# Output stages of a 1-core Trainium2 kernel: the last two weight units taken token half by token half, the norm behind them by halves too

## What is computed

```
first_block:                       # adaptive RMS norms, scale and shift from c
  h = rms(x) * (1 + scale) + shift;  x += gate * (hybrid_mixer(h) @ hyb_w_out)
  h = norm(x);                       x += gate * (swiglu(h) @ ffn_w_out[0])
  h = norm(x);                       x += gate * (retention(h) @ ret_w_out)
  h = norm(x);                       x += gate * (swiglu(h) @ ffn_w_out[1])
second_block, l = 0, 1:
  mix = concat(rms(y_lru), rms(y_nsa)) @ w_out[l]
  x = layer_norm(ALPHA * x + mix, ln1)
  x = layer_norm(ALPHA * x + peer(x), ln2)      # peer: 128 experts, out = sum_e c_e @ v_e
```

## Time and profile before

| what | value |
|---|---|
| profiled execution, its own time | 3087.28 us |
| its span | 3085.5 us |
| median of three runs | 3087.29 us |
| TensorE matmul busy | 2828.8 us (92%) |
| VectorE busy | 2225.6 us (72%) |
| ScalarE busy | 1604.9 us (52%) |
| mean granted TensorE clock | 0.954 of full |

### The profile page before, as it was taken

The page is one execution under the profiler, slowest core; times in us unless marked ns, Lnnn a source line. Parts: engine busy times, 40 slices in busy tenths (PEclk is TensorE's granted clock), DMA queues, the critical chain, the costliest instruction groups (busy, mean ns, idle before and its releaser), DMA issues.

```text
span 3085.5 us, 46430 instructions
## 1 busy us (share of the span) xinstructions
PE 2828.8 (92%) x17816; PEld 2520.9 (82%) x17816; DVE 2225.6 (72%) x3602; ACT 1604.9 (52%) x2733; POOL 82.9 (3%) x141
## 2 busy tenths in 40 slices
PE   6888799899799997999999999989798999999997
PEld 3675599786699876989999888878698999988886
DVE  2753566676555555899898878874579998977887
ACT  2333244334344353467888554545445778855453
POOL 1000000010000200000000000020000000000000
PEclk8889899899899988999999999998799999999999
DMA  7323567576355623556656877763255656587775
GB/s 254 111 62 116 191 226 252 181 230 206 116 178 182 208 77 102 182 186 204 193 190 205 265 241 242 241 207 117 70 178 180 202 189 198 190 264 242 243 241 161
DMA packets 211610, 580.28 MB, mean 188 GB/s; under 512 B 24032, under 2 KB 87808, under 8 KB 210112
## 3 DMA queue, kind: packets, MB, share of 16 engines
q1 hardware_dynamic: 162704, 495.20, 50.4%
q0 software_dynamic: 12976, 49.60, 4.9%
q10 hardware_dynamic: 35712, 32.52, 3.1%
HBM read 541.57 MB, written 35.65 MB: 187 GB/s over the span
## 4 chain that ended last, share of the span: by engine, by line
PE 73%; DVE 17%; ACT 6%; issue 2%; DMA 1%; ACTq 0%; POOL 0%; DVEq 0%; POOLq 0%
PE psum L692 72%; DVE wr L1895 4%; DVE gmem L1895 4%; DVE oh_r L1895 3%; ACT gmem L1352 2%; DVE gmem L1898 2%; ACT wr L1352 2%; ACT crf L1352 1%; PE psum L735 1%; DVE xmem L1898 1%; ACT L1352 1%; DVE gmem L2663 1%; DVE gmem L2076 0%; ACT xmem L1352 0%; ACTq L1838 0%
## 5 line engine op out<-in xcount | busy, mean ns | idle before, releaser
L1895 DVE TENSOR_TENSOR wr<-raw,wr 128x1024 fp32r<-128x1024 f32 (+1 forms) x814 | 994.2, 1223 | 494.5 <-ACT wr L1352 492.6
L692 PE MATMUL psum<-xr,wr 128*128 128x256 f32 x10464 | 1314.4, 286 | 31.0 <-DVE wr L1895 14.8
L692 PEld LDWEIGHTS psum<-xr,wr 128*128 128x128 f32 x10464 | 1289.3, 195 | 44.9 <-DVE xr L1895 14.5
L1352 ACT ACTIVATE wr<-raw 128x1024 fp32r<-128x1024 f32 (+1 forms) x814 | 853.8, 1049 | 320.7 <-PE psum L692 271.5
L692 PE MATMUL psum<-wr,cr 128*128 128x512 f32 x3072 | 696.8, 389 | 3.0 <-DVE cr L1895 3.0
L692 PEld LDWEIGHTS psum<-wr,cr 128*128 128x128 f32 x3072 | 576.6, 188 | 122.7 <-ACT cr L1352 3.3
L1352 ACT ACTIVATE gmem<-psum 128x512 f32<-128x512 f32 (+2 forms) x307 | 162.0, 540 | 276.2 <-PE psum L692 242.4
L1352 ACT ACTIVATE cr<-xmem 128x256 fp32r<-128x256 f32 x256 | 107.2, 419 | 341.9 <-PE psum L692 339.9
L692 PE MATMUL psum<-wr,xr 128*128 128x512 f32 (+1 forms) x960 | 242.3, 410 | 21.0 <-DVE xr L1895 11.0
L692 PEld LDWEIGHTS psum<-wr,xr 128*128 128x128 f32 x960 | 184.5, 200 | 68.3 <-issue 15.0
L692 PE MATMUL psum<-gmem 128*128 128x128 f32 (+8 forms) x1352 | 196.1, 299 | 17.2 <-DVE gmem L1895 13.6
(11 more groups left out here) (143 smaller groups left out, 1652.8 us busy)
## 6 DMA issues: line engine op xcount, KB each, us to landing
raw<-in_uv SPq DMA_DIRECT2D x512, 512.0 KB, 4.8
raw<-in_ffn_in SPq DMA_DIRECT2D x88, 512.0 KB, 4.1
gs<-xmem ACTq DMA_DIRECT2D x248, 128.0 KB, 3.7
xmem<-gs SPq DMA_DIRECT2D x248, 128.0 KB, 4.5
raw<-in_ada_w SPq DMA_DIRECT2D x48, 512.0 KB, 4.0
gmem<-in_ada_w POOLq DMA_DIRECT2D x48, 512.0 KB, 4.7
raw<-in_ffn_out SPq DMA_DIRECT2D x44, 512.0 KB, 3.5
raw<-in_ret_a SPq DMA_DIRECT2D x32, 512.0 KB, 4.3
```

Source lines behind the costliest of these rows:

```text
L692: ins = pe.matmul(o, a, b, start=first and i == 0, stop=final and i == len(pairs) - 1, skip_group_check=skip)
L1352: return act.activation(o, a, func, **k)
L1895: return dve.tensor_tensor(o, a, b, op)
```

## The change

The last two units of each output stage are multiplied together by a new function: first both units for token half 0, then both for token half 1. After the first of these TensorE raises a new signal, "half". VectorE's `residual`, or the first part of `layer_norm`, takes half 0 on that signal and half 1 on the end of the last unit. Variance, root and reciprocal are done for each half by itself. In `ada_norm` the row is first multiplied by the scale row (tensor_tensor, no need of the root), then by the reciprocal with the shift added, in two pieces of 512, each of which TensorE can transpose. ScalarE loads the table of the square root some units before the end of the stage (`preload_act_table`) in `hybrid_out`, `ffn_out_` and `peer_v`. VectorE's `split()` of the last unit's step goes behind the norm as `split(0)`, and so do the two clearings. The output is written by two DMAs.

```diff
+        def out_last(b, c_of, ks, sig):
+            pair = [(k, *next_unit()) for k in ks]
+            for a in range(2):
+                for k, j, hi, lo in pair:
+                    for n in range(2):
+                        e = slice(512 * n, 512 * n + 512)
+                        ch, cl = c_of(k)
+                        ins = mm3(bank(b + 2 * a + n), [(ch[:, quarter(a)], cl[:, quarter(a)], hi[:, e], lo[:, e])],
+                                  False, k == ks[1], True)
+                    if a:
+                        ins.then_inc(*W.pe.up(j))
+                    elif k == ks[1]:
+                        ins.then_inc(*X.pe.up(("half", sig)))
...
@@ tensor_program @@
         def hybrid_out(k):
-            out_unit(0, xr, k, 0, 8)
+            if k < 6:
+                out_unit(0, xr, k, 0, 8)
+            elif k == 6:
+                out_last(0, rows_of(xr), (6, 7), "hyb out")
...
         def peer_v(l, e):
+            c = e % 2
+            if e == NEXP - 2:
+                pe.wait_ge(*X.dve["c", l, NEXP - 1])
+                out_last(0, lambda k: (ccr[:, k % 2, 0, :], ccr[:, k % 2, 1, :]), (NEXP - 2, NEXP - 1), ("l2", l))
+            if e >= NEXP - 2:
+                return
...
         def mix_start(l):
-                    pe.wait_ge(*X.dve["ffn out", 1, 3])
                     for g in range(2):
+                        pe.wait_ge(*X.dve["ffn out", 1, 2 * a + g])
...
@@ scalar_program @@
         def ada_norm(tag):
             for a in range(2):
+                if name:
+                    act.wait_ge(*X.dve[(*name, 2 * a + 1)])
                 f(h[:, a, :], x[:, a, :], AF.Square, accum_out=ss[:, a:a + 1]).then_inc(*N.act.up((tag, "sq", a)))
-            root(N, tag, ss)
+            for a in range(2):
+                act.wait_ge(*N.dve[tag, "var", a])
+                f(ss[:, a:a + 1], ss[:, a:a + 1], AF.Sqrt).then_inc(*N.act.up((tag, "root", a)))
...
@@ vector_program @@
         def ada_norm(tag):
+            for a in range(2):
+                v = ss[:, a:a + 1]
+                dve.wait_ge(*N.act[tag, "sq", a])
+                ts(v, v, 1.0 / D, EPS, ALU.mult, ALU.add).then_inc(*N.dve.up((tag, "var", a)))
+                tt(h[:, a, :], x[:, a, :], aa, ALU.mult).then_inc(*N.dve.up())
+                dve.wait_ge(*N.act[tag, "root", a])
+                dve.reciprocal(v, v).then_inc(*N.dve.up())
                 own(N)
+                for g in range(2):
+                    e = slice(512 * g, 512 * g + 512)
+                    stt(h[:, a, e], h[:, a, e], v, sh[:, e], ALU.mult, ALU.add).then_inc(*N.dve.up((tag, "h", a, g)))
             for a in range(2):
                 for g in range(2):
                     lo_of(tag, xr, a, g, 4 + 2 * a + g)
+            if tag == ("ffn", 0):
+                zero(ff_b, [P, 2, 512]).then_inc(*A.dve.up(("zero", 0)))
...
+            if tag != "hyb":
+                split(0)
...
+        def residual(name, gt, tmp):
+            ahead.step()
+            for a in range(2):
+                dve.wait_ge(*(done() if a else X.pe["half", name]))
...
         def layer_norm(tag, src, g, b_, split_):
+            for a in range(2):
+                dve.wait_ge(*(done() if a else X.pe["half", tag]))
...
+                own(X)
                 for i in range(2):
                     dve.bn_stats(st[:, a, 6 * i:6 * i + 6], src[:, a, 512 * i:512 * i + 512]).then_inc(*N.dve.up())
...
+                ts(mv[:, 2 * a + 1:2 * a + 2], mv[:, 2 * a + 1:2 * a + 2], 1.0, LN_EPS, ALU.mult,
+                   ALU.add).then_inc(*N.dve.up((tag, "var", a)))
+            for a in range(2):
+                dve.wait_ge(*N.act[tag, "root", a])
+                dve.reciprocal(mv[:, 2 * a + 1:2 * a + 2], mv[:, 2 * a + 1:2 * a + 2]).then_inc(*N.dve.up())
...
@@ sync_program @@
+        for a in range(2):
+            sp.wait_ge(*N.dve[("l2", 1), "x", a])
+            sp.dma_start(out[128 * a:128 * a + 128, :], x[:, a, :]).then_inc(out_sem, 16)
```

More of the change, by code:

```diff
@@ L107, in call @@
         return self
-    wait_ge = matmul = transpose = activation = memset = tensor_tensor = tensor_scalar = call
+    wait_ge = matmul = transpose = activation = memset = tensor_tensor = tensor_scalar = preload_act_table = call
     scalar_tensor_tensor = tensor_copy = reciprocal = tensor_reduce = bn_stats = bn_aggr = call
@@ L318, in __init__, with step @@
             self.unit, self.next = -1, 0
+        def step(self):
+            self.unit += 1
         def to_split(self, step=1):
@@ L1074, in ret_out_ @@
                 claim(0, 1, 2, 3)
-            out_unit(0, oT, k, 0, 16)
+            if k < 14:
+                out_unit(0, oT, k, 0, 16)
+            elif k == 14:
+                out_last(0, rows_of(oT), (14, 15), "ret out")
             for i in range(4):
@@ L1558, in hybrid_out @@
             split()
+            if k == 4:
+                act.preload_act_table(AF.Sqrt)
         def mods(part):
@@ L1769, in layer_norm @@
         def layer_norm(tag, src, g, b_, split_):
-            root(N, tag, small_v[:, 24:28].rearrange("p (a s) -> p a s", s=2)[:, :, 1])
+            for a in range(2):
+                v = small_v[:, 25 + 2 * a:26 + 2 * a]
+                act.wait_ge(*N.dve[tag, "var", a])
+                f(v, v, AF.Sqrt).then_inc(*N.act.up((tag, "root", a)))
             if split_:
@@ L2028, in ada_norm @@
                     lo_of(tag, xr, a, g, 4 + 2 * a + g)
[L2030 to L2033, removed]
+            if tag == ("ffn", 0):
+                zero(ff_b, [P, 2, 512]).then_inc(*A.dve.up(("zero", 0)))
+            if tag == "ret":
+                zero(re_b, [P, 2, 512]).then_inc(*A.dve.up(("zero", 1)))
+            if tag != "hyb":
+                split(0)
         def qkv_(p, i):
@@ L2245, in hybrid_out @@
         def hybrid_out(k):
-            split()
-            if k == 7:
-                residual("hyb out", top(0), hy_tmp, done())
+            if k < 7:
+                split()
+            else:
+                residual("hyb out", top(0), hy_tmp)
         def mods(part):
@@ L2289, in ffn_out_ @@
         def ffn_out_(l, k):
-            split()
-            if k == FM - 1:
+            if k < FM - 1:
+                split()
+            else:
                 if l:
                     dve.wait_ge(*A.act["row", 11])
-                residual(("ffn out", l), top(3 if l == 0 else 9), ff_h, done())
+                residual(("ffn out", l), top(3 if l == 0 else 9), ff_h)
         def ret_qk(p, i):
@@ L2356, in ret_out_ @@
         def ret_out_(k):
-            split()
-            if k == 15:
-                residual("ret out", top(6), re_tmp, done())
+            if k < 15:
+                split()
+            else:
+                residual("ret out", top(6), re_tmp)
         def mix_start(l):
@@ L2533, in mix_out @@
         def mix_out(l, k):
-            split()
-            if k == 7:
-                dve.wait_ge(*done())
-                dve.wait_ge(*S.dve[("on", l), "rstd"])
-                for i in range(4):
-                    a = i // 2
-                    v = my[:, a, 512 * (i % 2):512 * (i % 2) + 512]
-                    stt(v, bank(2 + i), rn[:, 2 + a:3 + a], v, ALU.mult, ALU.add).then_inc(*X.dve.up(("mix out", l, i)))
+            if k < 7:
+                split()
         def layer_norm(tag, src, g, b_, split_):
@@ L2743, in peer_v @@
                 halve(l, e + 1)
-            split()
+                split()
         def peer_end(l):
-            dve.wait_ge(*done())
-            dve.wait_ge(ln2_in[l], 48)
-            for i in range(4):
-                a, e = i // 2, slice(512 * (i % 2), 512 * (i % 2) + 512)
-                stt(x[:, a, e], xo[:, a, e], ALPHA, bank(i), ALU.mult, ALU.add).then_inc(*X.dve.up(("y", l, i)))
+            pass
         order({"prologue": prologue, "modulate": modulate, "ada_norm": ada_norm, "qkv": qkv_, "conv": conv,
```

57 lines of the change are left out of this document (32 added, 25 removed).

## The result

The changed kernel takes 3065.83 us (median of five executions, 3064.67 to 3068.6). The kernel before has a median of 3100.83 over five executions (3086.4, 3087.29, 3100.83, 3103.18, 3104.34), three of them the ones that the prediction had. The ratio over all these executions is 0.9904, with a 95% interval of 0.9874 to 0.9933 (the quotient of the two medians would be 0.9887). So the change is faster by about 1%, but its time lies above the range of 3050 to 3064: the forecast was 3056.7. The profiled execution of the kernel after took 3065.82, span 3064.0, against a span of 3085.5 before. From profile to profile the change gives 21.5 us where the sum had 30.6.

What follows compares the result with a forecast made beforehand. Mostly TensorE matmuls (73% of the chain of waits); winnable time lies in joints, as long as VectorE's chain. 17.1 + 5.2 + 4.4 + 2.6 + 0.9 + 0.4 = 30.6 off 3087.3 gives 3056.7 us; range 3050 to 3064.

Steps and rivals of the forecast that it cites:

- joint 1: Gap behind the first output stage: first transposes at T + 5.1, TensorE restarts at T + 11.6 instead of 16.9, gain 5.3.
- output's DMA: Behind joint 8: the last DMA carries 512 KB and not 1 MB, gain 0.9, between 0.6 and 2.05.
- first norm: Order by halves adds a pass over the row but lets transposes start by pieces: gain 0.4, bounds 0 and 0.8.
- wait in `peer_v`: Ahead of joints 6 and 8: TensorE's pair waits for the multiplier of unit 127, 1.0 us lost in each.
- pair in the other joints: No cost to TensorE: 0.3 us to spare in joints 1 to 4, some 0.1 in joints 5 and 7.
- the 0.1 that was left out: Joints 1 to 3: uncertainty of the three-operand 512 piece, 0.65 to 0.68, 0.1 per joint, taken at the lower end.
- I take both, they cancel: Clock at two restarts: joint 4 probably stays at full clock, 1.6 gained; joint 6 falls to 0.50, 1.6 lost.
- The clock is kept: Rival: shorter gaps leave TensorE at full clock at four more restarts, 6.4 less, 3050 us; chance 0.12.
- ScalarE in VectorE's place: Rival: ScalarE's queue or a lost table preload delays joints 1 to 3 by 1.28 each, 3060.5 us; chance 0.08.
- Late loads: Rival: raw and `aux` loads fall together behind the joint, 0.7 to 1.9 in seven joints, 3062 to 3070; chance 0.08.
- Half 0 not overlapped: Rival: VectorE comes late to the signal, seven halves of 2.7 missing, 19 more, 3075.7 us; chance 0.06.
- The restart starves: Rival: the load released by deferred `split(0)` comes too late for units 5 and 6, 3103 us; chance 0.03.

Runs made afterwards that it cites:

- experiment 6: Changed kernel without the three preloads of the square root's table: median 3069.97 us, ratio 0.9905 to the kernel before.
- experiment 1: The kernel before, unedited, measured and profiled once more: median 3099.31 us over 12 executions, ratio 0.9996.
- experiment 7: Changed kernel plus unread TensorE products in the waits of joints 1 to 3 and 5 to 7, nine or twelve ahead of the transposes: median 3066.98 us.
- the same, late waits (8): experiment 7 plus, in the pair, later waits for the last `peer_v` multiplier and the second unit's lo part: median 3064.88 us, ratio 0.9887.
- Experiment 9: The kernel of (8) with fewer unread products, five or six ahead of the transposes, sized by the measured call: median 3046.54 us, ratio 0.9836.
- experiment 5: Changed kernel with VectorE's `split()` put back in front of the residual and the norm: median 3092.72 us, ratio 0.9988.
- experiment 3: Changed kernel with the wait for the last `peer_v` multiplier moved from ahead of the pair to between its two units: median 3064.78 us.

## Why the prediction was wrong

**The joints were right.** They should give 30.6 and gave 31.6. Each term of the sum against what the two profiles show, in us (a gap is from T to the next stage's first product):

| step | forecast gap | measured gap | forecast gain | measured gain |
|---|---|---|---|---|
| joint 1 | 11.6 | 11.20 | 5.3 | 5.69 |
| joint 2 | 11.6 | 11.20 | 6.4 | 6.76 |
| joint 3 | 11.6 | 11.20 | 5.4 | 5.85 |
| joint 4 | 5.4 | 5.39 | 5.2 | 5.24 |
| joints 5, 7 | 12.7 | 12.5, 12.9 | 2.2 + 2.2 | 2.37 + 2.01 |
| joints 6, 8, gap alone | | 12.2 | 2.3 + 2.3 | 2.35 + 2.35 |
| output's DMA | | 3.05 to land | 0.9 | 1.45 |
| first norm | | 13.6 | 0.4 | 1.08 |
| wait in `peer_v` | | 1.35 each | -1.0 - 1.0 | -1.35 - 1.35 |
| pair in the other joints | | | 0 | -0.8 |
| sum | | | 30.6 | 31.6 |

Half 0 was taken beside the pair, the first transposes came at T + 5.10 (forecast T + 5.1), joint 2 has no table load, and joints 5 and 7 are within 0.2 of the forecast. The wait in `peer_v` shows 1.02 idle, but from the end of unit 125 to T it is 6.79 instead of 5.44: a third of a microsecond comes on top of what stands as idle. From the end of the unit before to T it took 5.67 in joints 5 and 7, so the 0.1 to spare there was not enough, by 0.2; and it took 5.53 in joints 1 to 4, where the prediction had no cost: 0.8 in all. Three gains were put too low: the output's DMA went more by size than the nearest row said, the lo parts of joints 1 to 3 ended 0.4 earlier, and the first norm gave 1.1 and not 0.4. Against the Trainium skill's rule on small tiles that the prediction weighed (VectorE: DVE Perf Modes, TRN2 errata), the trace has 1.42 for two three-operand pieces, 0.14 above a whole row's 1.28 and near the 0.16 that the prediction worked out by that page; for the subtraction it was 1.28 against 1.22, 0.06. So the 0.1 that was left out was real, and small.

**The step that failed is the one on the clock**: "I take both, they cancel". It put the clock at nothing for the whole kernel after looking at two restarts, and set the sum against the base of 3087.3 as if the clock in it were any execution's. What was said of joints 4 and 6 came out in both profiles of the kernel after: joint 4 restarts at full clock, joint 6 at half (3.2 us behind the restart; these answer to the earlier trace rows). In experiment 6, whose joint 4 is the same, it restarts at 0.50, so even that isn't fixed.

```profile
1026.82:1030.00 3.18, 3.18 (x26) 3.18 (x27) 2.21 (x2) 0.00 (x0) 3.18 (x7) 1.00 0.93 368
...
2043.76:2047.00 3.24, 3.24 (x15) 3.24 (x16) 2.21 (x2) 0.16 (x1) 2.70 (x6) 0.50 1.03 435
```

But I looked at the clock only at the restarts. Within the stages the granted clock also falls, and how much work lies in such stretches differs from one execution to the next. The next table has, in us, each profile's joints and tail, what lies between the joints, and TensorE's busy time added up over all stretches with a granted clock of 0.50:

| profile | span | joints 1 to 7 and tail | between the joints | busy at 0.50 between | busy at 0.50 in all |
|---|---|---|---|---|---|
| before, of the prediction | 3085.5 | 122.6 | 2898.9 | 148.7 | 183.1 |
| before, once more (1) | 3099.4 | 122.7 | 2913.3 | 185.9 | 220.6 |
| after | 3064.0 | 88.5 | 2911.3 | 173.3 | 205.2 |
| after, once more (2) | 3065.2 | 88.5 | 2913.7 | 180.8 | 211.2 |
| after, unread products too long (7) | 3066.7 | 101.6 | 2901.6 | 152.3 | 160.2 |
| the same, late waits (8) | 3063.6 | 101.6 | 2896.5 | 150.4 | 159.1 |
| the same, sized (9) | 3044.3 | 85.4 | 2895.2 | 143.3 | 150.3 |
| before, unread products (10) | 3078.1 | 117.9 | 2895.6 | 145.9 | 156.1 |

The sum of 31.6 less the 21.5 seen leaves 10.1 us. Of these 8.8 lie between the joints (12.3 less the pair's 3.5) and 1.3 ahead of the first product, which comes 0.3 later though the norm in front of it is 1.1 shorter. Behind a restart TensorE did 15 matmuls in 3.2 us at 0.50 and 26 at 1.00, so half of the time at 0.50 is an estimate of what the clock costs; it turns out a high one. From the first profile of before to that of after it gives (173.3 - 148.7) / 2 = 12.3 between the joints, where 8.8 was measured; from before to before once more 18.6, where the same kernel got 14.3 longer. The Trainium skill (TensorE: Matmul & The Clock Gate, HAM oscillation) takes the penalty as half of the throttled time too; the trace agrees with the direction and has about three quarters of it in these two pairs. The Trainium skill (TensorE: Matmul & The Clock Gate, Part 1) puts the penalty of the warm-up ramp under 1% of a typical span. Here the work at half clock comes back behind many waits, and by half of it the estimate is 183 / 2 = 92 us of 3085, 3%, and in experiment 1 110.

The profile of before had less work at half clock than its own repetition and than both profiles of after. It came from the quicker third of the executions, and the median of three that stood beside it (3087.29) had two of that third. The kernel after has no second group. The sum of 30.6 was therefore set against a base that the typical execution doesn't have: against 3098.28, the median of the 17 executions of the kernel before beside experiment 1, it would have given 3067.7, inside after's eleven executions, 3063.5 to 3069.8. That the forecast's own ratio, 3056.7 / 3087.3 = 0.990, is the measured one is luck and no merit of the clock step: the median of before rose from 3087.29 to 3100.83 with two more executions. The warning was in the three times given, 3086.4, 3087.29 and 3103.18: one lay 16 us off, half of the forecast gain, and I let it pass.

**The rivals.** "The clock is kept" had the right subject and the wrong sign for this pair of profiles; six of the seven restarts are still at 0.50. What it said of cold matmuls that differ between runs of one kernel should have widened the range, and not by 1.6 for a restart but by the work inside the stages: some 14 us between two executions of one kernel. ScalarE in VectorE's place is out: no table load stands in joint 2, and the transposes start when VectorE's own steps in the sum say. Late loads are out: in joint 1 the clearing and both deferred `split()` end at 385.54, 2.8 us after the restart, TensorE has no second wait within 10 us of any of the seven restarts, and it isn't idle more between the joints (132.8 against 133.0). "Half 0 not overlapped" is out for the change itself; experiment 5 shows what it costs when it happens, 26.8 us and not the 19 of the rival, because the `split()` in front adds 1 us to each joint. "The restart starves" is out.

**What stays open.** Experiment 9's profile is 19.7 below that of the kernel after: its joints are 3.1 shorter (eight transposes of joint 1 take 1.32 instead of 1.97), and 16.1 come from between the joints, of which 3.5 are the pair's waits. The 12.6 left are near the estimate from the clock, (173.3 - 143.3) / 2 = 15.0. The late waits without unread products were not run by themselves. Why less was measured than half of the time at 0.50, from 0.72 of it (before to after) to 0.92 (after to experiment 7), was not taken apart. Why the kernel before has two groups of times is shown only so far: they differ in how much work lies at half clock, and in six executions with the waits filled neither came up. That the kernel after has one group rests on eleven executions; with one wait moved (experiment 3) six times fell into two and four, 4 us apart. What puts one execution into one group was not tried.

## What to carry to other kernels

Take a forecast's base from several executions, and compare profiles stretch by stretch: the same matmuls with more busy time are the clock, and neither the change nor the joints. An overlap is worth only as much as the instruction standing in front of it on its engine lets through; here moving one subtraction behind the norm decided over 27 of 33 us. Where TensorE must wait for a few microseconds, unread products that fit the wait, sized by the measured duration of one, were worth some 16 us on top of the change's 33; sized too long they were worth nothing.

## What the runs showed of the hardware

- Filling TensorE's waits in the seven joints of the kernel before, and nothing else, took it from 3098 to 3081.7 and its spread from 17 us to 2.7. In the kernel after, filling six of them (all but 4) together with the late waits took the work at half clock from 205 to 150 us and the time from 3065.9 to 3046.5.
- One float32 product of 128 x 128 by 512 columns is two records of TensorE and 0.88 to 0.89 us (18 records in 7.88, 10 in 4.45). I had sized experiment 7 with half of that.
- A single-core kernel with nothing random in it has two groups of times, some 13 us apart (22 of 62 at 3086.4 to 3091.4, 40 at 3096.7 to 3104.3). The idle times of its joints agree to 0.01 us between the two profiles, one of each group; the difference is in how long the same matmuls take.
- Behind a wait of 1.02 that shows as idle, TensorE was 1.35 later at the end of its next 24 matmuls (6.79 from the end of the unit before, 5.44 without a wait). So this wait cost 0.33 more than the idle time shown.
